# Probability tiles turned by TensorE's transpose instead of a matmul with a diagonal of inverse sums

## What is computed

```python
# MLA: one map per head
s = jnp.einsum('bqhd,bkhd->bhqk', qi, k).astype(jnp.float32) * scale
p = jax.nn.softmax(jnp.where(mask, s, NEG_INF), axis=-1).astype(v.dtype)
o = jnp.einsum('bhqk,bkhd->bqhd', p, v)

# differential attention: two maps per head, a scalar lam per layer
a = jax.nn.softmax(jnp.where(mask, sc, NEG_INF), axis=-1)
p = (a[:, :, 0] - lam * a[:, :, 1]).astype(v.dtype)
o = jnp.einsum('bhqk,bkhd->bqhd', p, v)
```

## Time and profile before

| | |
|---|---|
| three runs | 1744.55, 1745.17, 1749.18 us; median 1745.17 |
| span of the profiled execution | 1748.7 us |
| its own time | not listed by itself; the largest of the three, 1749.18, lies 0.5 us above the span |
| mean granted TensorE clock | 0.979 of full speed |
| TensorE busy | 1645.5 us, 94% |
| VectorE busy | 1117.7 us, 64% |
| ScalarE busy | 705.8 us, 40% |
| GpSimd busy | 227.8 us, 13% |
| DMA | mean 91 GB/s |

### The profile page before, as it was taken

One profiled execution on the slowest core, in us unless ns is written; L12 is line 12 of the kernel. 1 busy time (PEld: TensorE's weight loads), 2 busy tenths in 40 slices (PEclk: granted clock), 3 DMA queues, 4 the chain that ended last, 5 costly groups with the idle time before them and its releaser, 6 DMA issues. The chain is left out here.

```text
span 1748.7 us, 22087 instructions
## 1 busy us (share of the span) xinstructions
PE 1645.5 (94%) x7472; PEld 1284.5 (73%) x7472; DVE 1117.7 (64%) x1604; ACT 705.8 (40%) x1082; POOL 227.8 (13%) x212
## 2 busy tenths in 40 slices
PE   6889989999999999999988999999999999999996
PEld 4467686578767888888866768567867788888874
DVE  8967973775345764764775886475444675575576
ACT  3232445663334432432443344664243442342343
POOL 6410501112012000000020151111102000000002
PEclk8989999999999999999998999999999999999998
DMA  3143143322212332333224223331312232232323
GB/s 135 48 153 96 61 122 96 103 61 93 82 37 85 96 96 97 96 97 96 90 79 142 85 73 121 91 115 49 97 49 61 86 97 94 96 98 95 97 83 109
DMA packets 50048, 159.69 MB, mean 91 GB/s; under 512 B 6576, under 2 KB 6832, under 8 KB 49072
## 3 DMA queue, kind: packets, MB, share of 16 engines
q1 hardware_dynamic: 49968, 158.63, 29.4%
HBM read 144.97 MB, written 7.34 MB: 87 GB/s over the span
## 5 line engine op out<-in xcount | busy, mean ns | idle before, releaser
L661 ACT ACTIVATE wh<-raw 128x1024 fp32r<-128x1024 f32 x246 | 260.5, 1060 | 659.0 <-PE psum L1221 646.5
L1219 PE MATMUL psum<-a_hi,wh 128*128 128x512 f32 x1072 | 423.4, 395 | 7.9 <-DVE wl L913 7.3
L913 DVE TENSOR_TENSOR wl<-raw,wh 128x1024 fp32r<-128x1024 f32 x246 | 302.7, 1231 | 187.3 <-ACT wh L661 187.1
L1221 PE MATMUL psum<-a_hi,wl 128*128 128x512 f32 x1072 | 419.9, 392 | 0.0
L1220 PE MATMUL psum<-a_lo,wh 128*128 128x512 f32 x1072 | 419.9, 392 | 0.0
L1219 PEld LDWEIGHTS psum<-a_hi,wh 128*128 128x128 f32 x1072 | 203.0, 189 | 57.1 <-DVE wl L913 12.3
L1219 PE MATMUL psum<-b_hi,wh 128*128 128x512 f32 x608 | 239.6, 394 | 5.6 <-DVE wl L913 2.5
L1220 PE MATMUL psum<-b_lo,wh 128*128 128x512 f32 x608 | 236.8, 389 | 0.0
L1221 PE MATMUL psum<-b_hi,wl 128*128 128x512 f32 x608 | 236.6, 389 | 0.0
L1220 PEld LDWEIGHTS psum<-a_lo,wh 128*128 128x128 f32 x1072 | 203.1, 189 | 43.4 <-issue 1.4
L1221 PEld LDWEIGHTS psum<-a_hi,wl 128*128 128x128 f32 x1072 | 202.8, 189 | 42.7
(11 more groups left out here) (209 smaller groups left out, 2171.1 us busy)
## 6 DMA issues: line engine op xcount, KB each, us to landing
raw<-in_w_main SPq DMA_DIRECT2D x106, 512.0 KB, 3.5
raw<-in_w_up SPq DMA_DIRECT2D x88, 512.0 KB, 3.5
raw<-in_w_down SPq DMA_DIRECT2D x32, 512.0 KB, 3.5
bias<-bias_scratch SPq DMA_DIRECT2D x32, 256.0 KB, 2.9
terms<-qk SPq DMA_DIRECT2D x48, 128.0 KB, 2.4
raw<-in_w_last SPq DMA_DIRECT2D x16, 384.0 KB, 3.0
bias_scratch<-stage SPq DMA_DIRECT2D x64, 64.0 KB, 1.6
raw<-in_w_first SPq DMA_DIRECT2D x6, 512.0 KB, 3.5
```

The lines of the kernel that those rows point to most:

```text
L661: act.activation(wh[:, b].rearrange("p k m -> p (k m)")[:, 0:width], raw[:, b, 0:width], ACT.Copy).then_inc(w_hi, 1)
L913: dve.tensor_tensor(wl[:, b].rearrange("p k m -> p (k m)"), raw[:, b, :], wh[:, b].rearrange("p k m -> p (k m)").bitcast(F32), ALU.subtrac ...
L1219: pe.matmul(out_ap, wh[:, b, k, :], his[:, k, :], start=(begin and i == 0), stop=False)
L1221: last = pe.matmul(out_ap, wl[:, b, k, :], his[:, k, :], start=False, stop=(end and i == len(tiles) - 1))
```

## The change

GpSimd's loop over diagonals and the tile `diag` are taken out. For an MLA tile VectorE, after the reciprocal, waits for it and multiplies the tile's rows by the inverse sums in place. For a differential pair it multiplies the first map's rows by their inverse sums, makes the weight from the second map's inverse sum and lam alone, waits for the scaling, and adds the second map as before. TensorE waits for one semaphore, `p_normed`, in place of `diag_in` and `p_ready`, and uses its transpose with the identity.

```diff
@@ gpsimd
-                    for u in range(32):
-                        if u >= 4:
-                            pool.wait_ge(t_full, u - 3)
-                        m = u if u < 16 else 2 * u - 16
-                        pool.wait_ge(rec_in, u + 1)
-                        pool.tensor_scalar(diag[:, u % 4, :], ident, rec[:, m:m + 1], None, ALU.mult).then_inc(diag_in, 1)
@@ vector, 1 <= t < 17
                             dve.reciprocal(rec[:, m:m + 1], sums[:, m:m + 1]).then_inc(rec_in, 1)
+                            dve.wait_ge(rec_in, m + 1)
+                            e = ering[:, m % RING, :]
+                            dve.tensor_scalar(e, e, rec[:, m:m + 1], None, ALU.mult).then_inc(p_normed, 1)
@@ vector, 17 <= t < 33
                             dve.wait_ge(rec_in, 16 + u + 1)
-                            step(dve.scalar_tensor_tensor(wgt[:, u:u + 1], rec[:, k + 1:k + 2], lam[:, 4:5],
-                                                          sums[:, k:k + 1], ALU.mult, ALU.mult))
-                            dve.scalar_tensor_tensor(e0, e1, wgt[:, u:u + 1], e0, ALU.mult, ALU.add).then_inc(p_ready, 1)
+                            dve.tensor_scalar(e0, e0, rec[:, k:k + 1], None, ALU.mult).then_inc(p_ready, 1)
+                            step(dve.tensor_scalar(wgt[:, u:u + 1], rec[:, k + 1:k + 2], lam[:, 4:5], None, ALU.mult))
+                            dve.wait_ge(p_ready, u + 1)
+                            dve.scalar_tensor_tensor(e0, e1, wgt[:, u:u + 1], e0, ALU.mult, ALU.add).then_inc(p_normed, 1)
@@ tensor, turn(u, e)
-                        pe.wait_ge(diag_in, u + 1)
-                        if u >= 16:
-                            pe.wait_ge(p_ready, u - 16 + 1)
+                        pe.wait_ge(p_normed, u + 1)
                         if u >= 2:
                             pe.wait_ge(t_free, u - 1)
                         for kb in range(4):
-                            last = pe.matmul(TR[u % 2][:, P * kb:P * kb + P], e[:, P * kb:P * kb + P], diag[:, u % 4, :],
-                                             start=True, stop=True)
+                            last = pe.transpose(TR[u % 2][:, P * kb:P * kb + P], e[:, P * kb:P * kb + P], ident)
                         last.then_inc(t_full, 1)
```

More of the change, by code:

```diff
@@ L214, in qm @@
             return (qm01 if h < 2 else qm23)[:, h % 2, :]
-        diag, _ = sb("diag", [P, 4, P], F32, ssum_at)
         mem0, _ = sb("mem0", [P, KT, M], F32, qc_at)
@@ L273, in block_program @@
         bias_in = [sem(f"bias_in{i}") for i in range(4)]
-        rec_in, diag_in = sem("inverse_sums_in"), sem("diagonal_in")
+        rec_in, p_normed = sem("inverse_sums_in"), sem("p_normalised")
         sub_sq, sub_out = sem("sub_squared"), sem("sub_normed")
```

## The result

The changed kernel takes 1751.0 us (median of 9 runs, 1749.51 to 1756.75) against 1747.86 for the kernel before (9 runs beside them, 1743.06 to 1749.56). The ratio is 1.0025, with a 95% interval of 1.0013 to 1.0037: about 4 us slower by the ratio (the medians lie 3.1 us apart), less than the 0.3% that the forecast had set as the bound of what can be told. The forecast was 1748, the range 1741 to 1757.

The account below looks back on a forecast made before the run. In the attention stage, VectorE's chains rather than TensorE (94% busy) were taken to decide nearly everywhere; shorter turns against added scalings summed to +2.9 us over two layers, added to the 1745.17 us median: 1748, range 1741 to 1757.

Parts of the forecast that it names:

- The scaling: VectorE's added 128x512 multiplication per turn: 484 ns taken (range ends 477 and 910), 0.40 us of its queue.
- Rival A: Slower: the scaling takes 622 ns, or its waits cost as much: 1753 us, at 910 ns 1764; chance 0.22.
- The turns: TensorE's 64 tile transposes: four records in place of eight, 0.60 us for 1.06, each taken as 0.45 us shorter.
- E: Transposing fp32 tiles takes two passes here too, so about five turns a layer give nothing: 1752.5 us; chance 0.04.
- The ring: Attention steps 1 to 7: ScalarE and VectorE chain of 4.62 us, growing 0.52 a step; -0.10 us after it.
- B: A little faster: ScalarE's and VectorE's order has missed slack, six turns count: -2.7 us a layer, 1743; chance 0.13.
- Steps 8 to 11: Attention steps of TensorE alone: turns at two steps lie in its chain before the first MLA product, -0.90 us.
- Steps 12 to 17: VectorE's, then ScalarE's chain: two scalings add 1.04 us, partly absorbed by a 0.55 us wait: +0.41 us.
- Steps 18 to 27: Regular pair steps: VectorE needs 2.78 us a step against 2.64; on the marks +0.75 us.
- Steps 28 to 35: Attention stage's end: VectorE saturated in steps 29 to 32 (+1.6 us), last turn 0.45 shorter; on the marks +1.35.
- C: TensorE bounds everywhere, so all 64 shorter turns count, 28.8 us: 1716 us; chance 0.03.
- D: TensorE's activity drops and its clock halves in some 12 steps a layer: 38 us in all, 1786; chance 0.05.

Follow-up runs that it names:

- the early fills: Changed kernel with spare 128x512 products in TensorE's long waits of attention steps 14 and 17 alone: 1751.92 us, 1.0030 against the kernel before.
- the late fills: Changed kernel with spare 128x512 products in TensorE's long waits of attention steps 29, 32 and 33 alone: 1748.65 us, 1.0007 against the kernel before.
- the MLA half: Kernel before with the change for each layer's 16 MLA tiles alone, pairs keeping the diagonal: 1744.56 against 1749.32 us, 0.9977.
- the pair half: Kernel before with the change for each layer's 16 pairs alone, MLA tiles keeping the diagonal: 1750.24 us, 1.0005.

## Why the prediction was right, and where its steps were not

The time and the verdict held, and so did the core of the mechanism: VectorE can't take the scaling for free, and that eats what the shorter turns give. The runs show it from three sides: 1.0% faster without the scaling, 0.7% slower with the scaling alone, 1.1% slower again when it is done twice. The agreement of the sum (+1.5 us a layer against +2.2 and +1.5) is partly luck. The work came out about 2 us a layer cheaper than summed, and something that was left at nothing, by the profiles the clock, gave it back. The time agrees for one more reason of that kind: the sum was added to a median of 1745.17 us, and the kernel before has 1747.86 in the comparison. As a difference, +2.9 us were forecast, and +3.1 (medians) or +4.4 (ratio) measured.

- **The scaling** was taken at 484 ns and measured 486; two rows of other shapes priced it well. The 133 ns in the sum's upper value is not what the rows give (a quarter of 541 ns is 135, so 486), which changes nothing. By the table in the Trainium skill, "VectorE: DVE Perf Modes", section on the TRN2 errata, it would have been 327 ns, an estimate; the text below that table says that its row is too low and that the fixed part measured about 150 cycles (on a bf16 copy), not 58, which makes 423 ns, an estimate too. The trace is above both and decides. Rival A (622 ns or more) falls. The combination got 0.03 us cheaper, where a few hundredths had been weighed against the extra wait.
- **The turns** are four records, 0.60 to 0.66 us: E falls.
- **The ring closes**, as forecast: no idle time before the weight split, TensorE waiting 0.66 us. B falls. But "-0.10" after the ring was -1.2 (S to M). A step grew by 0.43 us, not 0.52. And the start of the ring had a loss that I had not read: before, TensorE waited 2.33 us for its first diagonal at 256.71, that turn took 1.63 us, and the window from 254 to 262 had a granted clock of 0.79 (the only fall of that stage, in both layers); in the changed kernel it is 1.00 and TensorE waits 1.25 us there. At the split of 263.81 the forecast was +0.17 us from S; measured -0.37.
- **Steps 8 to 11**: two turns in TensorE's chain, -0.90. Three are between the marks: -1.37 at the full clock (14.52 to 13.15 us), but +0.30 when the clock falls behind the wait of 2.74 us.
- **Steps 12 to 17**: +0.41, measured +0.84 and +0.82 (V to A). VectorE's chain absorbs less there than the wait of 0.55 us promised. The slow products are not part of it: with the early fills, where they run at full speed, V to A is the same 21.1 us.
- **Steps 18 to 27**: +0.75, measured +0.09. The pace was 2.78 us and came out as 2.73, so six steps cost 0.56 us and not 0.84; and more than one turn ahead of step 19 was still on TensorE's path: from A to the scores at 336.92 are 14.03 us against 14.65 to those at 337.25.
- **Steps 28 to 35**: +1.35. With the late waits filled it is +1.16 (21.73 against 20.57), so the forecast of VectorE's work was good. Unfilled it is +2.18 and +3.17. This is the step that failed in size: in these profiles TensorE's clock fell behind waits that are longer than before, and the stretch is 1.0 and 2.0 us longer than with the late fills.
- **C**, TensorE as the only bound, falls by far: all 64 short turns with no scaling and no diagonals at all are 1.0% (17.5 us), not 28.8.
- **D** was the rival with the right place and the wrong mechanism. It expected the regular steps to be too idle and asked 38 us. Those steps kept the clock. It fell behind single long waits. My line that a granted clock under 1.00 in steps 19 to 32 would make the forecast wrong by D was too coarse: it came true (0.62 at 360 to 369 us) and went with 1 to 2 us a layer.

Summed from the table at the full clock the change would be -1.2 - 1.4 + 0.8 + 0.1 + 1.2 = -0.5 us a layer, no change to speak of (the -1.2 still holds the fall that the kernel before had at its first diagonal). That the measured loss is the clock is supported by the mean clocks and by the late fills (1.0007), but it is not shown: no kernel here was free of every fall, the fills add work of their own, the early fills don't fit, the changed kernel was measured in one comparison only, and one profile of each kernel is a sample of where the clock falls. The stretch between the two stages, the same program in all of them, lasts 677.7 to 681.9 us in the 14 profiles, which is as much as the effect, so single spans can't tell these kernels apart.

## What to carry to other kernels

Moving work from the busiest engine by count to another pays only where that other engine isn't already the one that is waited for; look for the idle time step by step and choose the engine for each step (ScalarE at 722 ns in idle time beat VectorE at 486 in a chain). Costs and gains that were measured one at a time need not add up. Behind a wait that a faster TensorE gains, the work that follows may run at half speed, and then the wait costs more than its length; ask whether that work is covered before filling or removing the wait. Before comparing two profiles part by part, look at one stretch in several executions, or the clock's luck is read as the change's effect.

## What the runs showed of the hardware that had not been expected

- The granted clock (levels 2.4 and 1.2 GHz) fell to the lower one behind single waits of TensorE of 1.44, 1.86, 2.12, 2.14, 2.33 and 2.74 us. Behind three of these it fell in one layer or execution and not in another: 1.45 us at 1178.88, 2.12 us at 1135.97 and 2.74 us (all above). It stayed up behind 1.48 us (the turn at 375.20 and the products after it) and 1.90 us too (the products at 322.60 before, 3.62 us for eight records) and behind 2.12 us at the first turn of the kernel with ScalarE's scaling (257.24, 0.66 us). The length of the wait alone doesn't decide; what else does was not found.
- The combination takes 785 ns where GpSimd builds a diagonal beside it (before, and in the MLA half 780) and 752 when GpSimd is silent (after, and in the pair half). In the kernel with both scaling and diagonals, the diagonal falls on other operations:
```profile
341.38 0.83 POOL L650 TENSOR_SCALAR diag<-cst,rec 128x128 f32<-128x128 f32 x1 [2.03 <-DVE rec L1065]
...
341.25 0.49 DVE L1068 TENSOR_SCALAR ering<-ering,rec 128x512 f32<-128x512 f32 x1
341.65 0.33 DVE L1069 SCALAR_TENSOR_TENSOR wgt<-rec,lam,sums 128x1 f32<-128x1 f32 x1
342.02 0.75 DVE L1072 SCALAR_TENSOR_TENSOR ering<-ering,wgt 128x512 f32<-128x512 f32 x1
```
  Now the pairs' diagonal takes 0.83 us instead of 0.60, the tiny weight 0.33 instead of 0.22, and the combination is at 0.75; the scaling beside it keeps its 0.49. That the two engines slow each other by some 0.03 to 0.2 us where they meet is read from which operations overlap; no run moved one of them alone.
